# The input projection of a hybrid attention layer: another order for the head norms, the latent projections and their gains

## Time and profile before

| what | value |
|---|---|
| median of 3 runs | 1766.95 us (1766.26 to 1776.94) |
| the profiled execution | 1766.95 us |
| its span, first to last instruction | 1764.8 us |
| mean granted clock of PE over the span | 0.983 |
| PE busy | 1688.9 us, 96% of the span |
| DVE, ACT, POOL busy | 958.6, 423.9, 1019.5 us |
| the stage of the change | from about 377 us to 496 us of the span |

### The profile page before, as it was taken

The page is one execution under the profiler, slowest core; times in us unless marked ns, Lnnn a source line. Parts: engine busy times, 40 slices in busy tenths (PEclk is TensorE's granted clock), DMA queues, the critical chain, the costliest instruction groups (busy, mean ns, idle before and its releaser), DMA issues.

```text
span 1764.8 us, 26693 instructions
## 1 busy us (share of the span) xinstructions
PE 1688.9 (96%) x10162; PEld 1371.7 (78%) x10162; DVE 958.6 (54%) x1392; ACT 423.9 (24%) x696; POOL 1019.5 (58%) x606
## 2 busy tenths in 40 slices
PE   7999999999989999999999999989999999999996
PEld 5888888887755678888888776878877888888885
DVE  5666662227566347565542268977744675666012
ACT  4000000017855321111100131324441333333000
POOL 3666667766577567766677644630005366666675
PEclk9999999999999999999999899999999799999998
DMA  5444443332220134444443322310003132233332
GB/s 195 147 143 143 144 146 116 107 121 85 82 71 2 48 102 143 147 138 143 145 152 105 99 72 72 96 37 3 3 2 96 44 99 95 95 95 95 108 107 95
DMA packets 48797, 173.75 MB, mean 98 GB/s; under 512 B 5424, under 2 KB 5808, under 8 KB 48464
## 3 DMA queue, kind: packets, MB, share of 16 engines
q1 hardware_dynamic: 39888, 143.00, 24.9%
q10 hardware_dynamic: 8832, 29.63, 5.1%
HBM read 170.51 MB, written 2.10 MB: 98 GB/s over the span
## 4 chain that ended last, share of the span: by engine, by line
PE 86%; DVE 8%; ACT 2%; POOL 2%; issue 2%; DMA 0%; POOLq 0%; SPq 0%; DVEq 0%; ACTq 0%
PE banks L551 24%; PE banks L552 24%; PE banks L553 24%; PE banks L918 4%; PE banks L599 2%; DVE banks L1929 2%; POOL prob L502 1%; PE banks L819 1%; PE banks L805 1%; PE banks L893 1%; PE banks L593 0%; PE banks L592 0%; PE banks L594 0%; PE banks L790 0%; PE banks L794 0%
## 5 line engine op out<-in xcount | busy, mean ns | idle before, releaser
L493 POOL TENSOR_SCALAR w_hi<-w_raw 128x1024 fp32r<-128x1024 f32 x260 | 295.0, 1135 | 671.9 <-DMA w_raw<-in_slabs 671.4
L495 POOL TENSOR_TENSOR w_lo<-w_raw,w_hi 128x1024 fp32r<-128x1024 f32 x260 | 643.6, 2475 | 21.7
L551 PE MATMUL banks<-h_hi,w_hi 128*128 128x512 f32 x1464 | 576.6, 394 | 20.6 <-DVE w_lo L1716 12.8
L552 PE MATMUL banks<-h_lo,w_hi 128*128 128x512 f32 x1464 | 571.8, 391 | 0.0
L553 PE MATMUL banks<-h_hi,w_lo 128*128 128x512 f32 x1464 | 571.7, 390 | 0.0
L551 PEld LDWEIGHTS banks<-h_hi,w_hi 128*128 128x128 f32 x1464 | 276.2, 189 | 84.0 <-issue 25.5
L553 PEld LDWEIGHTS banks<-h_hi,w_lo 128*128 128x128 f32 x1464 | 276.2, 189 | 58.1
L552 PEld LDWEIGHTS banks<-h_lo,w_hi 128*128 128x128 f32 x1464 | 276.5, 189 | 57.7 <-issue 1.2
L551 PE MATMUL banks<-act_hi,w_hi 128*128 128x512 f32 x528 | 205.4, 389 | 0.0
L552 PE MATMUL banks<-act_lo,w_hi 128*128 128x512 f32 x528 | 205.4, 389 | 0.0
L553 PE MATMUL banks<-act_hi,w_lo 128*128 128x512 f32 x528 | 205.4, 389 | 0.0
(11 more groups left out here) (309 smaller groups left out, 1744.5 us busy)
## 6 DMA issues: line engine op xcount, KB each, us to landing
w_raw<-in_slabs SPq DMA_DIRECT2D x264, 512.0 KB, 3.5
adaw<-in_ada ACTq DMA_DIRECT2D x48, 512.0 KB, 4.0
xT<-in_x SPq DMA_DIRECT2D x2, 1024.0 KB, 7.1
relb<-in_relb ACTq DMA_DIRECT2D x8, 256.0 KB, 2.9
out_y<-xT SPq DMA_DIRECT2D x8, 256.0 KB, 2.0
block<-in_block ACTq DMA_DIRECT2D x1, 704.0 KB, 6.1
silc<-in_ada ACTq DMA_DIRECT2D x1, 512.0 KB, 5.1
tmp<-in_rope ACTq DMA_DIRECT2D x1, 512.0 KB, 4.3
```

What stands on the lines that cost most here:

```text
L493: nc.gpsimd.tensor_scalar(w_hi[:, r, :], w_raw[:, r, :], 1.0, 1.0, ALU.mult, ALU.mult).then_inc(S("w_hi"), 1)
L495: nc.gpsimd.tensor_tensor(w_lo[:, r, :], w_raw[:, r, :], w_hi[:, r, :], ALU.subtract).then_inc(S("w_split"), 1)
L551: mm(out, hi, rhs_hi, start=start, stop=False, skip_group_check=True)
L552: mm(out, hi, rhs_lo, start=False, stop=False, skip_group_check=True)
```

```diff
-IN1_ORDER = [0, 1, 2, 3, 4, 5, "uq0", 6, 7, "uq1", 8, 9, "ukv", 10, 11, 12, 13, 14, 15]
+IN1_ORDER = [0, 1, 2, 3, 4, 5, "uq0", 6, "uq1", 7, "ukv", 8, 9, 10, 11, 12, 13, 14, 15]
...
-SUMS_AFTER = {"kr0": ["cq0", "cq1"], "qa0": ["ckv0", "kr0"], "qn0": ["qa0"], "qa2": ["qa1", "qn0"], "qa3": ["qn1", "qn2"],
...
-LOGS_AFTER = {"ckv0": ["cq1"], "qa0": ["ckv0", "kr0"], "qa1": ["qa0"], "qa2": ["qa1", "qn0"], "qa3": ["qn1"],
...
+SUMS_AFTER = {2: ["cq0", "cq1"], 3: ["ckv0"], 4: ["kr0"], 5: ["qa0"], "uq0": ["qa1"], 6: ["qn0", "qn1", "qn2"], "uq1": ["qa2"],
+              "kn3": ["qn3", "qr0", "qr1", "qa3"], 9: ["kn0", "kn1", "kn2", "kn3"], 12: ["ka0", "ka1", "ka2", "ka3"]}
+ROOTS_AFTER = {2: ["cq1"], 4: ["ckv0", "kr0"], "uq0": ["qa0", "qa1"], "uq1": ["qn0", "qn1", "qn2", "qa2"],
+               "ukv": SUMS_AFTER["kn3"], 9: SUMS_AFTER[9], 12: SUMS_AFTER[12]}
+APPLIED_AFTER = {3: ["cq0", "cq1"], 5: ["ckv0", "kr0"], 6: ["qa0", "qa1"], 7: ["qn0", "qn1", "qn2", "qa2"],
+                 8: SUMS_AFTER["kn3"], 10: SUMS_AFTER[9], 12: SUMS_AFTER[12]}
+
+LOWS_AFTER = {8: [], 9: ["ka0", "ka1"], 10: [], 11: ["ka3"], "kn": ["ka2"]}
...
-                if j == 10:
-                    pe.wait_ge(S("hd_applied"), len(NORMED))
-                else:
+                if j > 10:
                     pe.wait_ge(S("roped"), j - 10)
...
-            late_norm(10)
             scores(0)
...
-                if 12 <= i <= 13:
+                if 11 <= i <= 13:
                     late_norm(i - 1)
...
+            for unit in IN1_ORDER[:16]:
+                for name in names_of(unit):
+                    if name in NORMED:
+                        head_square(name)
+                head_roots(ROOTS_AFTER.get(unit, []))
...
-                for name in names:
+                for i, name in enumerate(names):
                     head_raw(name, unit)
...
+                    if i >= 1 and names[i - 1] in NORMED:
+                        head_lo(names[i - 1])
+                for name in LOWS_AFTER.get(unit, names[-1:]):
+                    if name in NORMED:
+                        head_lo(name)
+                for name in APPLIED_AFTER.get(unit, []):
+                    head_apply(name)
```

More of the change, by code:

```diff
@@ L144, in names_of @@
     return LATENTS.get(unit, [IN1_NAMES[unit]] if unit in range(12) else [])
-SUMS_AFTER = {"kr0": ["cq0", "cq1"], "qa0": ["ckv0", "kr0"], "qn0": ["qa0"], "qa2": ["qa1", "qn0"], "qa3": ["qn1", "qn2"],
-              "qn3": ["qa2"], "ka0": ["qa3", "qn3"], "ka1": ["qr0", "qr1"], "kn1": ["ka0"], "ka2": ["ka1"],
-              "ka3": ["kn0", "kn1", "kn2"], "va0": ["kn3"], "va1": ["ka2", "ka3"]}
-LOGS_AFTER = {"ckv0": ["cq1"], "qa0": ["ckv0", "kr0"], "qa1": ["qa0"], "qa2": ["qa1", "qn0"], "qa3": ["qn1"],
-              "qn3": ["qn2", "qa2"], "ka0": ["qa3", "qn3"], "ka1": ["qr0"], "kn2": ["qr1", "ka0"], "kn3": ["ka1"],
-              "ka3": ["kn0", "kn1", "kn2"], "va": ["kn3", "ka2", "ka3"]}
-ROOTS_AFTER = {"kr0": ["cq1"], "qa0": ["ckv0", "kr0"], "qn2": ["qa0"], "qa2": ["qa1", "qn0"], "qn3": ["qn1"],
-               "qr1": ["qn2", "qa2"], "ka0": ["qa3", "qn3"], "kn2": ["qr0", "qr1", "ka0"], "kn3": ["ka1"],
-               "ka3": ["kn0", "kn1", "kn2"], "va": ["kn3", "ka2", "ka3"]}
-LOWS_AFTER = {"cq1": ["cq0", "cq1"], "ckv0": ["ckv0"], "kr0": ["kr0"], "qa0": ["qa0"], "qn0": ["qa1"], "qn2": ["qn0", "qn1", "qn2"],
-              "qa2": ["qa2"], "qa3": ["qa3"], "qr0": ["qn3"], "qr1": ["qr0", "qr1"], "ka0": ["ka0"], "ka1": ["ka1"],
-              "vb3": ["kn0", "kn1", "kn2"], "ka2": ["kn3"], "ka3": ["ka2", "ka3"]}
-APPLIED_AFTER = {"kr0": ["cq0", "cq1"], "qn1": ["ckv0"], "qa2": ["kr0", "qa0"], "qa3": ["qa1", "qn0"], "qr1": ["qn1"],
-                 "ka0": ["qn2", "qa2"], "ka1": ["qa3", "qn3"], "vb3": ["qr0", "qr1", "ka0"], "ka3": ["ka1"],
-                 "va": ["kn0", "kn1", "kn2", "kn3", "ka2", "ka3"]}
+SUMS_AFTER = {2: ["cq0", "cq1"], 3: ["ckv0"], 4: ["kr0"], 5: ["qa0"], "uq0": ["qa1"], 6: ["qn0", "qn1", "qn2"], "uq1": ["qa2"],
[5 more added lines that the diff above has]
+LOWS_AFTER = {8: [], 9: ["ka0", "ka1"], 10: [], 11: ["ka3"], "kn": ["ka2"]}
 def constants():
@@ L737, in _ @@
                         latent(name, unit, i)
-                        for done in SUMS_AFTER.get(name, []):
-                            head_stat(done)
+                        if name == "kn3":
+                            for done in SUMS_AFTER["kn3"]:
+                                head_stat(done)
                 elif unit < 12:
@@ L1762, in _ @@
                 names = names_of(unit)
[L1763 removed]
+                for i, name in enumerate(names):
                     head_raw(name, unit)
[L1765 to L1777 removed]
+                    if i >= 1 and names[i - 1] in NORMED:
[5 more added lines that the diff above has]
+                    head_apply(name)
+                if unit == 10:
+                    for name in LOWS_AFTER["kn"]:
+                        head_lo(name)
+                if unit == 3:
+                    dve.wait_ge(S("hd_applied"), 2)
+                    for k in range(2):
+                        split_latent(cq[:, k, :], cq_hi[:, k, :], cq_lo[:, k, :])
+                if unit == 5:
+                    dve.wait_ge(S("hd_applied"), 3)
+                    split_latent(ckv[:, 0, :], ckv_hi[:, 0, :], ckv_lo[:, 0, :])
             for t in (2, 3, 0, 1):
```

29 lines of the change are left out of this document (5 added, 24 removed).

## The result

The changed kernel takes 1789.8 us (median of 4 runs, 1789.33 to 1789.96) against 1768.7 us for the kernel before (median of 4 runs); the ratio is 1.011 with a 95% interval of 1.0077 to 1.0145. That is 14 to 26 us slower, and the median of 1789.8 us lies within the range of 1774 to 1791 around the forecast of 1783 us, near its upper end. The profiled execution of the change took 1786.25 us where that of the kernel before took 1766.95, its span is 1784.2 us, and the mean granted clock 0.977 where it was 0.983.

What follows compares the result with a forecast made beforehand. PE, busy for 96% of the span, was taken to bound the kernel. Waits 9.1, collisions 5, clock 1.5 and swap 0.5 sum to 16.1 us on 1766.95: 1783 us, range 1774 to 1791.

Steps and rivals of the forecast that it cites:

- heavier: Rival: nearly every DVE-POOL collision counts and the clock falls at two waits; +21.6 us, 1788.5 us; chance 0.35.
- Place A: Statistics of qn0 to qn2, together behind qa2: PE waits for qa0 to be applied; 5.8 us.
- Place B: Statistics inside "ukv": PE waits 2.7 us for qn0 to be applied, then 0.8 for DVE's pace; 3.5 us.
- Place C: Rest of "ukv": DVE's eight operations take 6 us against PE's 3.6, and ka0 needs vb0's bank; 2.4 us.
- Place D: Statistic of cq1: a low part that waits for ACT now stands between two evictions; 1.0 us.
- Sum without collisions: Stage: 12.7 us of waits at four places and 0.8 for restarts, less the 4.4 of before; +9.1 us.
- Collisions: Stage: DVE's low parts and splits slowed beside POOL's splits; +5 us, half of a possible 10.4.
- The clock: Stage: the granted clock falls once, behind a long wait of PE; +1.5 us, bounds 0 and twice that.
- The swap: Swap matmul moved from ahead of the first scores to step 11, where it costs PE time; +0.5 us.
- Behind the stage: Sign: the mechanism is wrong if the loss shows in the attention behind the stage.
- Table loads: Sign: ACT should have 14 table loads in the stage, of 20 before.
- not slower: Rival: six table loads fewer, 7.7 us of ACT, so no statistic waits any more; 1762.5 us; chance 0.02.

Runs made afterwards that it cites:

- the second profile: The changed kernel run once more as it is, on the chip of the experiments; ratio 1.0102 to the kernel before, stage 129.89 us.
- group_a_only: Kernel before, three tables changed for qa0 to qn2: their statistics together behind qa2, Ln and Exp of qa0 and qa1 as one group; ratio 1.0090.
- quiet_after: Changed kernel, POOL making only 8 of 1024 columns of each weights' low part in the stage, PE using the high part instead; ratio 1.0055.
- quiet_before: Kernel before, POOL making only 8 of 1024 columns of each weights' low part in the stage, PE using the high part instead; ratio 0.9981.
- tiles_new: Kernel before with the change's order of units and five new tables keyed by tiles, most statistics asked for later; ratio 0.9978.
- tiles_old: Kernel before, its order of units kept, with other tables that ask for statistics one to three tiles later; ratio 0.9957.

## Why the prediction was right, point by point

**Which of its cases came.** The forecast was +16.1 us, and the measured +19.3 us of the profiled executions (1786.25 - 1766.95) and +21.1 of the medians (1789.80 - 1768.74) lie beyond the +17.7 at which the prediction drew the line to its "heavier" case, to which it gave 0.35 and 1788.5 us. That case asked for two things. The clock fell at A and again at B, as it says, but the collisions counted for little (1.3 to 3.9 us, where it has 9). So the range was right and the place within it was not: the mechanism is the forecast's, with the step for the clock too small and that for the collisions too large, as told below.

**The bound.** It said that only PE's waits in its stage can gain or lose. 15.5 of 19.4 us are there in the first pair of profiles: 10.3 of waits, 4.2 of the clock behind them, and 1.0 of the rest.

**Place A, 5.8 us.** Measured 5.69, 7.27 in the second profile, and 6.56 without POOL's low parts. The chain was foreseen instruction by instruction, and L1740 ended the wait at 437.9 us, within the 430 to 440 said. That 5.69 is so close to the 5.8 is in part luck: the 5.8 is a sum without collisions, for which 6.56 is the measurement, and with them PE had already waited 1.77 us at 431.55 for a low part of the statistic just before, which the prediction had no term for. In group_a_only, in the old order of units, the same chain cost 3.28 us at its place, and the rest of the 14.5 us came at others.

**Place B, 3.5 us.** It is 2.7 us of wait and 0.8 of pacing. The wait measured 3.13 and 3.08 us, and 3.13 without the low parts. The pacing is no term of its own: the four statistics came 0.85 to 1.02 us apart, at the lower clock, and are counted there.

**Place C, 2.4 us.** Too high: 0.2 us in the first profile of after and 0.7 + 0.5 = 1.2 in the second. DVE's eight operations took the 6.0 us that the step gave them (458.36 to 464.34 us in after). But the step took PE's five tiles at full pace, and PE came slowly from place B, with its matmuls 0.43 us apart until 462.65, so that DVE gained on it.

**Place D, 1.0 us.** 2.10 us, with POOL beside the low part, and 0.95 without (quiet_after). The term was right and the collision fell on it.

**Sum without collisions, +9.1.** The quiet pair measures 8.9 us of waits and 1.7 of restarts and pacing, 10.6. Here too errors met: the waits of the change were put at 12.7 with the pacing and are 11.4, and the 4.4 of before are 2.5 in quiet_before.

**Collisions, +5.** Measured 1.3 to 3.9 us, with the doubt said above, at the lower edge of what the prediction allowed ("if the collisions add less than 2 or more than 9 us"). What failed is that it let the 4.4 us of before go whole and then added collisions: the quiet kernel before has 2.5 us of waits, so before's own collisions, 2.4 to 2.6 us of its stage, had to be taken off. They also did not fall where it put them, on the chain of place A alone: the waits for low parts, 5.7 us with collisions and 1.0 without, stand at three places.

**The clock, +1.5 for one fall.** This is the term that was mis-sized. The clock fell at A and at B: in the first profile 8 starts 0.42 or 0.43 us apart behind A and 13 behind B, 21 x 0.2 = 4.2 us, above the bound of 3; in the second 8 and 5, 2.6 us. The error is that it counted one fall, though it had foreseen two waits. And before, which it took to keep its clock, had a fall of its own in its second profile, with 6 such starts.

**The swap, +0.5.** Nothing that can be seen: after's distance to before stayed at +16.1 us from the first scores (513.47 and 497.40) to past step 13, where its matmuls now are 547.11 and were 531.01.

**Behind the stage, nothing.** It said it would be wrong on the mechanism if the loss showed in the attention behind. It does not. But 1.2 to 3.3 us lie further behind, in the feed-forward and the second block, where the programs are the same, and the prediction had no term for them.

**Table loads.** 14 as said (7 and 7), six fewer than before:

```profile
L1305 ACT ACT_TABLE_LOAD x7 | 9.0, 1283 | 0.1
L1308 ACT ACT_TABLE_LOAD x7 | 9.0, 1283 | 0.1
```

They free 6 x 1.283 = 7.7 us of ACT, and PE gains nothing from it. The rival "not slower" rested on them and fell. The Trainium skill has the rule to group activations by table set and to do all of one set before switching ("ScalarE: Activation LUTs", Rules for kernel authors). This case's traces agree that it saves loads, 14 in place of 20, but the time did not follow: tiles_new with 16 loads and tiles_old with 18 are faster than the changed kernel with 14 by 1.0102 - 0.9978 and 1.0102 - 0.9957, 22 and 26 us.

So the total of +16.1 was near the 19.4 us of the profiles and the 14 to 26 us of the timed runs because its errors went both ways: collisions and place C too high, the clock and what lies behind the stage too low. That much of it is luck.

## What to carry to other kernels

Where a result goes round several engines in a few buffers, a result that is asked for early, or made in a group behind other work, makes every engine wait in turn, whatever the grouping saves on one of them. The size of a group is not the whole of it: tiles_new takes four Exp in one group, on four banks, and PE waits for none of these norms. No run varied the group's size or the lateness of the statistics alone. Follow that ring before counting saved table loads, and ask for results some tiles later, as tiles_new and tiles_old do, which changed more than that; a wait removed at one place of the ring is in large part waited at the next, so judge by the length of the stage and not by the wait. And count a fall of the clock behind each larger wait of PE as well: here it cost 2.6 to 4.2 us in all, 15 to 27% of the loss in the stage.
